# Gate and up projections of a fused transformer step in seven block products instead of eight, with the sums of weight blocks made by GpSimd

## What is computed

```
mix = W_o( sigmoid(gate_a) * W_pa(o_a) + sigmoid(gate_b) * W_pb(o_d) )
x   = x + gate1 * mix
h2  = RMSNorm(x) * g2 * (1 + scale2) + shift2
ffn = (silu(h2 @ w_gate) * (h2 @ w_up)) @ w_down        # w_gate, w_up: 1024 x 2816, w_down: 2816 x 1024
y   = x + gate2 * ffn
```

## Time and profile before

| | |
|---|---|
| three runs, us | 2876.12, 2865.03, 2870.81, median 2870.81 |
| profiled execution, span | 2868.7 us (2.1 us under that median) |
| PE busy | 2667.2 us, 93% |
| DVE, ACT, POOL busy | 1377.7, 1051.3, 654.1 us |
| mix_out | 1669.7 to 1926.5 us |
| feed_forward | 1926.85 us to the end |

### The profile page before, as it was taken

The page is one execution under the profiler, slowest core; times in us unless marked ns, Lnnn a source line. Parts: engine busy times, 40 slices in busy tenths (PEclk is TensorE's granted clock), DMA queues, the critical chain, the costliest instruction groups (busy, mean ns, idle before and its releaser), DMA issues. The chain is left out here.

```text
span 2868.7 us, 46254 instructions
## 1 busy us (share of the span) xinstructions
PE 2667.2 (93%) x18134; PEld 2513.3 (88%) x18134; DVE 1377.7 (48%) x2236; ACT 1051.3 (37%) x1845; POOL 654.1 (23%) x577
## 2 busy tenths in 40 slices
PE   7999999889998999948999989899999999999999
PEld 3898999778888888836887779899999999999999
DVE  3565332156765777557888834442222242222221
ACT  4322333234333443236888833322222222222211
POOL 1000222433433434143335441201111000111100
PEclk9999999879986999859999999999999999999999
DMA  5323665433444333141010045422222232222232
GB/s 208 140 88 108 206 224 180 142 100 90 108 112 127 105 90 105 41 159 49 16 62 17 9 145 200 143 74 74 75 78 73 90 111 87 73 77 76 71 93 72
DMA packets 197756, 294.26 MB, mean 103 GB/s; under 512 B 83376, under 2 KB 123344, under 8 KB 196048
## 3 DMA queue, kind: packets, MB, share of 16 engines
q1 hardware_dynamic: 194704, 276.18, 30.5%
q10 hardware_dynamic: 2880, 15.73, 1.6%
HBM read 228.32 MB, written 63.52 MB: 102 GB/s over the span
## 5 line engine op out<-in xcount | busy, mean ns | idle before, releaser
L277 PE MATMUL f_ps<-mf_h_hi,mf_w_hi 128*128 128x320 f32 x1408 | 434.8, 309 | 1.4 <-PEq L2076 1.4
L277 PE MATMUL f_ps<-mf_h_hi,mf_w_lo 128*128 128x320 f32 x1408 | 434.7, 309 | 0.0
L277 PE MATMUL f_ps<-mf_h_lo,mf_w_hi 128*128 128x320 f32 x1408 | 434.7, 309 | 0.0
L2510 DVE TENSOR_TENSOR mf_w_lo<-mf_w_raw,mf_w_hi 128x1024 fp32r<-128x1024 f32 (+1 forms) x135 | 188.9, 1399 | 421.0 <-ACT mf_w_hi L2362 420.7
L277 PE MATMUL proj_ps<-h_hi,w_hi 128*128 128x320 f32 x896 | 283.0, 316 | 6.0 <-DVE w_lo L571 5.6
L277 PE MATMUL proj_ps<-h_lo,w_hi 128*128 128x320 f32 x896 | 278.4, 311 | 0.0
L277 PE MATMUL proj_ps<-h_hi,w_lo 128*128 128x320 f32 x896 | 278.3, 311 | 0.0
L277 PEld LDWEIGHTS f_ps<-mf_h_hi,mf_w_hi 128*128 128x128 f32 x1408 | 264.7, 188 | 1.6 <-issue 1.6
L277 PEld LDWEIGHTS f_ps<-mf_h_lo,mf_w_hi 128*128 128x128 f32 x1408 | 264.7, 188 | 0.0
L277 PEld LDWEIGHTS f_ps<-mf_h_hi,mf_w_lo 128*128 128x128 f32 x1408 | 264.7, 188 | 0.0
L2436 POOL TENSOR_TENSOR f_ff_lo<-f_ff_f,f_ff_hi 128x640 f32 (+1 forms) x44 | 69.3, 1574 | 770.4 <-ACT f_ff_hi L2362 770.4
(11 more groups left out here) (343 smaller groups left out, 6539.2 us busy)
## 6 DMA issues: line engine op xcount, KB each, us to landing
mf_w_raw<-w_up_dram SPq DMA_DIRECT2D x88, 512.0 KB, 3.5
w_raw<-w_in_dram SPq DMA_DIRECT2D x48, 512.0 KB, 4.4
w_ada_raw<-w_ada_dram SPq DMA_DIRECT2D x16, 1024.0 KB, 5.0
mf_w_raw<-w_mix_dram SPq DMA_DIRECT2D x32, 512.0 KB, 5.1
mf_w_raw<-w_down_dram SPq DMA_DIRECT2D x32, 448.0 KB, 3.3
delta_t<-delta_tile ACTq DMA_DIRECT2D x10, 1024.0 KB, 6.8
decay_t<-g_rows SPq DMA_DIRECT2D x40, 256.0 KB, 4.6
kq_t<-delta_t SPq DMA_DIRECT2D x20, 512.0 KB, 4.1
```

The source lines that it names most:

```text
L277: ins = nc.tensor.matmul(out, w(k), a(k), start=(first and n == 0 and q == 0), stop=(last and n == len(ks) - 1 and q == 2))
L2510: nc.vector.tensor_tensor(wlo[:, slot, 0:nk], raw[:, slot, 0:nk], whi[:, slot, 0:nk].bitcast(F32), ALU.subtract).then_inc(E[half]["lo"], 1)
```

## The change

The gate and the up matrices of one tile f, stacked, are two block rows (up is row 1, gate row 2) by two halves of the 1024 channels; h2 is two halves of the channels by two groups of 320 tokens. Before, the eight block products are made. Now seven are, by Strassen's scheme in Winograd's form. Their weight operands, in order (`PRODUCTS`): `11`, `s2`, `s1`, `s3`, `12`, `22`, `s4`, with s1 = 21 + 22, s3 = 11 - 21, s2 = s1 - 11, s4 = 12 - s2. A product is 4 channel tiles by 3 matmuls, 12 matmuls of 320 columns, as before. In detail:

- **Steps.** A step n takes one f: 10 steps with the first half of the tokens alone (t = 0, f 0 to 9), 12 with both halves (f 10 to 21), 10 with the second half alone (f 0 to 9). All is unrolled. Step positions q = 7n + i, i being the product.
- **Banks.** Each t has banks A, C and two B used by turns. Products 0, 1, 3 and 5 of a step add up in one B bank. ScalarE copies it out after product 0 (`p1`) and after product 1 (`u2`); PE may begin product 1 only when the first copy is made, and product 3 only after the second. DVE adds `p1`, `u2` and the copy of C to later banks; PE begins product 5 after the sum of i = 3.
- **Weights.** Gate and up tile come in one transfer of 1 MB, two slots. GpSimd makes s1, s3, s2, s4 in place (128 x 512 each, L2228 of the new kernel). s2 overwrites `11` and waits until its low part is made; s4 does so for `12`. ScalarE and DVE split each of the seven operands, three positions ahead (`AHEAD`), into a ring of six.
- **Sums of h2** (`TokenSums`): four differences of 128 x 1280 by DVE, seven splits of 128 x 1280 (ScalarE high, DVE low), for the first half in units 24 to 30 of mix_out, for the second in the solo steps of the first, one piece every third position from q = 30 to 62; before that its tiles are scaled and shifted at q = 8, 11, ... 29.
- **Norms.** GpSimd adds the squares (`add_squares`), and PE makes one pair of float32 matmuls per half. In mix_out two tiles per unit are scaled and shifted in units 19 to 22. In feed_forward root and inverse are Ln and Exp on ScalarE.
- **f goes through DRAM.** SP stores f (`f_t`) and loads it again for the down product: tiles 0 to 13 of the first half during the last solo steps, tiles 14 to 21 when the last of the seven products is done. The second half's tiles come in three batches (8, 7, 7) during parts (m 7, c 1), (7, 2) and the first part of the second half; a batch is split only when all of it has landed (`loaded`), and its load waits for the batch before.
- mix_out ends with the split of the first three weight operands.

```diff
+UNITS_UP = FT
+SOLO = 10
+RING = 6
+AHEAD = 3
+PRODUCTS = ("11", "s2", "s1", "s3", "12", "22", "s4")
...
+    def high(self, act, q):
+        n, i = divmod(q, 7)
...
+            act.wait_ge(self.sum_ready, 4 * n + {"s1": 1, "s3": 2, "s2": 3, "s4": 4}[PRODUCTS[i]])
+        self.nc.scalar.activation(self.slot(q, 0), self.source(q), ACT.Copy).then_inc(self.hi_ready, 1)
...
+    def sum(self, pool, n, name):
+        q = 7 * n + {"s1": 0, "s3": 0, "s2": 0, "s4": PRODUCTS.index("12")}[name]
...
+        if name in ("s2", "s4"):
+            pool.wait_ge(self.lo_ready, q + 1)
...
+        self.nc.gpsimd.tensor_tensor(out, a, b, op).then_inc(self.sum_ready, 1)
...
             def sum_of_squares(m):
-                pe.wait_ge(e["x1_sq"], m + 1)
-                for g in range(2):
-                    last = nc.tensor.matmul(ps[1][:, 2 + g, 0:GN], keep["ones"][:], sq[:, m % 2, g * GN:(g + 1) * GN], start=(m == 0), stop=(m == KT - 1))
...
+                if u == NORM0:
+                    pe.wait_ge(e["sq_added"], KT - 1)
+                    for g in range(2):
+                        last = nc.tensor.matmul(ps[1][:, 2 + g, 0:GN], keep["ones"][:], acc[:, g * GN:(g + 1) * GN], start=True, stop=True)
...
+        STEPS = [(f, (0,)) for f in range(SOLO)] + [(f, (0, 1)) for f in range(SOLO, FT)] + [(f, (1,)) for f in range(SOLO)]
...
+        FIRST, SHIFT0, SUM0, EVERY = 2, 8, 32, 3
+        shift_at = {SHIFT0 + 3 * m: m for m in range(KT)}
+        low_at = {SUM0 + EVERY * j: name for j, name in enumerate(T_PIECES)}
+        split_at = {TAIL + 21 + 3 * k: k for k in range(14)}
+        GROUPS = (14, FT, FT + 8, FT + 15, 2 * FT)
+        AGAIN = {(0, KT - 1, 1): range(0, 8), (0, KT - 1, 2): range(8, 15), (1, 0, 0): range(15, 22)}
...
+                        if (half, m, c) in AGAIN:
+                            sp.wait_ge(d_done, part_no(half, m, c))
+                            sp.wait_ge(f_in, 16 * (FT + AGAIN[half, m, c][0]))
+                            for k in AGAIN[half, m, c]:
+                                load_f(1, k)
...
         @block.scalar
...
+            for q in range(7 * N):
...
+                    up.high(act, q + AHEAD)
...
+                if q in shift_at:
+                    act.wait_ge(scaled, m + 1)
...
+                    if i == 0:
+                        act.wait_ge(prod, index[n, i, t] + 1)
+                        cp(p1[t][:], b_bank(n, t)[:, 0:GN]).then_inc(p1_ready[t], 1)
...
+                    if i == 4:
+                        act.wait_ge(c22_ready[t], c + 1)
+                        nc.scalar.activation(sg[t][:, GN:HT], sg[t][:, GN:HT], ACT.Silu).then_inc(sig2[t], 1)
...
         @block.vector
...
+            for q in range(7 * N):
...
+                    up.low(dve, q + AHEAD)
...
+                    if i == 3:
+                        dve.wait_ge(prod, index[n, i, t] + 1)
+                        dve.wait_ge(p5_ready[t], c + 1)
+                        nc.vector.tensor_tensor(sg[t][:, GN:HT], b_bank(n, t)[:, 0:GN], sg[t][:, GN:HT], ALU.add).then_inc(c22_ready[t], 1)
...
         @block.tensor
...
+            def product(q, t):
...
+                out = (b_bank(n, t), b_bank(n, t), C[t], b_bank(n, t), A[t], b_bank(n, t), C[t])[i]
...
+                elif i == 1:
+                    pe.wait_ge(p1_ready[t], c + 1)
...
+                elif i == 3:
+                    pe.wait_ge(u2_ready[t], c + 1)
...
+                elif i == 5:
+                    pe.wait_ge(c22_ready[t], c + 1)
+                for k in range(T_HALF):
+                    for part, (wp, tp) in enumerate(((0, 0), (0, 1), (1, 0))):
+                        last = nc.tensor.matmul(out[:, 0:GN], up.slot(q, wp)[:, k], t_operand(w, t, PRODUCTS[i], tp)[:, k],
+                                                start=(i in (0, 2, 4) and k == 0 and part == 0), stop=(k == T_HALF - 1 and part == 2), skip_group_check=(i not in (0, 2, 4)))
```

838 lines of the change are left out of this document (512 added, 326 removed).

## The result

The changed kernel takes 2839.93 us (median of four runs, 2832.21 to 2842.97) where the kernel before takes 2868.81 us (four runs, 2865.03 to 2876.12): 0.9895 of it, with a 95% interval of 0.9876 to 0.9913. That is 28.9 us less; the prediction said 2820 us, inside 2796 to 2858. The sign and the range held, 20 us of the expected 49 us did not come.

The account below looks back on a forecast made before the run. PE alone was taken to bound feed_forward, at 0.1468 us per matmul. From a span of 2868.7 us, gains of 94.4 us and costs of 44 us gave 2818.3 us, so 2820 us for the median, range 2796 to 2858.

Parts of the forecast that it names:

- rival 5: Feed_forward: 3696 matmuls changing operand and bank every 12 run at 0.160 us, not 0.1468: +49 us, 2869 us; chance 0.04.
- Rival 4: Change of halves: loads of f run at half the rate, batches cost another 22 us: 2842 us; chance 0.08.
- mix_out in all: mix_out: fewer squares and no stand after unit 16, against longer units 19 to 22 and a weight split: -9.4 us.
- The copy after product 0: Solo steps: PE waits for ScalarE's bank copy before product 1, 0.75 us in each of 20 steps: 15 us.
- DVE and GpSimd in the first half's solo steps: First half's solo steps: the engines' turns at SBUF plus pieces exceed PE's time: 11 us (0 to 25).
- the start: Start of feed_forward, q = 4: ScalarE waits for the mean, does Ln and Exp, next copy late: 1.5 us (0 to 4).
- second rival: Solo steps: the s2 weight chain is late and delays the next copy, 2 us in each of 20: 2860 us; chance 0.12.
- third rival: Solo steps: GpSimd loses its SBUF turns, sums take 2.26 us instead of 1.29: +66 us, 2886 us; chance 0.04.
- The clock: Change of halves: after PE's stand the clock falls and PE works slower for some microseconds: 2 us.
- Second half's solo steps: Second half's solo steps: 14 splits of f on DVE fill the SBUF turns to 13 us: 3.5 us (0 to 10).
- Start of the down product: Into the down product: DVE's last work, then eight loaded tiles of f and weights 1.6 us late: 4 us (2.5 to 8).
- Change of halves: Between the down product's halves: three batches of f, weights queued behind splits, PE stands, clock falls: 9 us (3 to 18).

Follow-up runs that it names:

- full_nosums: "full" without GpSimd's sums of weight blocks, raw blocks in their place (result not the scheme's): 2781.8 us, 0.9704 of the kernel before.
- late: Changed kernel with side pieces (x1 scaling, sums, splits) queued behind the work PE waits for, x1's shift one position later: 2829.8 us, 0.9855 of the kernel before.
- nosums: Changed kernel without GpSimd's weight sums and the waits for them, raw blocks used (result not the scheme's): 2819.5 us, 0.9846 of the kernel before.
- full: Changed kernel with products reordered, side pieces later, weights split ahead of f, five f tiles early, eight f loads spread: 2787.0 us, 0.9730 of the kernel before.

## Why the prediction was right, and where it was off

*Right.* The pace: 528 matmuls fewer at 0.147 us, and no penalty for a change of bank every 12, in the 2016 matmuls of the shared steps and in the 756 of nine solo steps where PE waits for nothing (110.6 us in "full_nosums"); rival 5 is out. Rival 4 is not seen: between 2645 and 2685 us, where the batches of f land, the DMA moved 243 GB/s with its idle ends and up to 421. The norm pair after unit 16: from gates to gates 8.1 us, as forecast. The loop through three engines in units 19 to 22: 9.76 us, forecast 9.7. DVE's products of gates in the changed kernel, from unit 16 on, where the earlier trace rows had 15.56 and 8.43 us:

```profile
1785.53 1.56 DVE L2488 TENSOR_TENSOR mf_gates<-m_ps,mf_gates 128x640 f32<-128x640 f32 x2 [4.66 <-PE m_ps L277]
1793.65 1.56 DVE L2488 TENSOR_TENSOR mf_gates<-m_ps,mf_gates 128x640 f32<-128x640 f32 x2 [1.40 <-PE m_ps L277]
...
1811.97 1.54 DVE L2488 TENSOR_TENSOR mf_gates<-m_ps,mf_gates 128x640 f32<-128x640 f32 x2
1821.73 1.55 DVE L2488 TENSOR_TENSOR mf_gates<-m_ps,mf_gates 128x640 f32<-128x640 f32 x2
```

mix_out in all: -9.4 forecast, -6.8 in this profile, and -9.0 by the median of the thirteen profiles in the table (248.2 us).

*Off*, by 19.4 us in feed_forward, term by term:
- **The copy after product 0**: 15 us forecast, 0.75 us each. It cost 0.85 us where nothing stands beside it, 17 us for twenty.
- **DVE and GpSimd in the first half's solo steps**, with the start: 12.5 us forecast. The ten steps took 155.3 us; 123.3 are bare matmuls, 1.1 the pair for the norm, 8.5 ten copies, and 22.4 us are left. This step failed by its reasoning, not only by its size. It summed the turns over 30 positions and took what did not fit, and it priced single pieces that stand in front of PE's work at 1.2 to 2 us. "late" shows that their places alone cost 11.5 us in nine steps, "nosums" that the sums cost 17.3 us there (the two overlap). Of these 17.3 the late chain is 8.6 us; the second rival had priced it at 2 us in each of 20 steps. The sharing, which the sum had let fit in, is 8.7, with GpSimd's sums at 1.5 us, not the 2.26 of the third rival. I had given them as alternatives; they add.
- **The clock** was counted only for the change of halves, 2 us. Of the 22.4 us above it is 4.3: 2.8 after the stand of 3.28 us in the third step and 1.5 after one of 1.92 us before 2037.37 us. With the 2.9 and 3.5 us below that makes 10.7 us.
- **Second half's solo steps**: 3.5 us forecast for the splits of f; 135.5 - 123.3 - 8.5 = 3.7 us. That the size fits is partly luck. In four steps PE waits for DVE's sum, 2.5 us with the restarts: there a split of f stands in DVE's queue and low parts stretch beside GpSimd's sums. The other 1.2 us is the second step, where the next weights are late, and no term of mine had it (the lines stand below). Without GpSimd's sums, in "nosums", both are nothing.
- **Start of the down product**: 4 us forecast. The stands were of 2.7 and 2.2 us, where 2.5 and 1.6 were forecast; a clock of 0.87 over 22.1 us adds 2.9 us, 7.7 us in all.
- **Change of halves**: 9 us forecast; 9.4 us of stands and 0.92 over 43.7 us (3.5 us), 12.9 us. The first stand was 6.1 us where I had 4.7: the mechanism, weights queued behind eight splits, was the right one.

The misses add up: 2 + 9.9 + 0.2 + 3.7 + 3.9 = 19.7 us, where 19.4 are to be explained.

Late weights in the second half's second step (engine waited, us in total, times, longest):

```profile
POOL mf_s L2228 <- DMA mf_up_raw<-w_up_dram: 4.8, 1, 4.8
ACT mf_up_slots L2213 <- DMA mf_up_raw<-w_up_dram: 2.7, 1, 2.7
```

SP asked for these weights at 2370.86 us, right behind the fourteen loads of f, and they came at 2383.4 us; the sums, ScalarE's high parts and the next copy follow late, and PE stands 1.77 us for it, until 2390.30 us, in place of 0.62. DVE's wait for the store of f, which makes this step long in "full", is not in the changed kernel's list: the same loads stand ahead in both, of the weights here and of the store there. For the changed kernel this is read from the order on SP's queue alone; no run tried it.

Of the signs that the prediction had named, the waits for the copy came in 20 places, but at 20.5 us and not 15. The first half's steps were 15.5 us long in the mean, and four of nine took 16.1 to 19.8 us. That was named as the sign of rival 3, whose cause, sums of 2.26 us, was not there: the length of a step alone does not tell the rivals apart. And rival 3's own price, 2885 us less 2820 over 20 solo steps, is 3.25 us a step, not the 3.6 given there.

## What to carry to other kernels

When a scheme saves work on the bound engine by making its results depend on evacuations, order its products so that no two neighbours need the same bank: here the order of seven names in a tuple was worth 22 us of a 77 us saving. An in-order engine's average load says little; a side job costs what stands behind it, so put it behind the work that the bound engine waits for, and put a batch of loads where neither a store that frees a buffer nor the next weights queue behind it. An engine that "only" takes sums off another's hands is not free where the two share SBUF.
